# Four layer norms: squares summed around an early mean, drift taken out later, and the first two weight blocks behind each interleaved

## The chip, the cores and the metric

The kernel runs on one core of one Trainium2 chip. The metric is the device time of one execution in microseconds. The time of the kernel before is the median of three runs; the trace is that of one further execution, run with the hardware profiler.

## What is computed

Two transformer blocks over 512 tokens of width 1024, in float32. The change touches the four layer norms of the first block: one behind each mixer and one behind each feed-forward network, in two layers.

```python
def layer_norm(x, g, b):
    xf = x.astype(jnp.float32)
    mu = jnp.mean(xf, axis=-1, keepdims=True)
    var = jnp.mean(jnp.square(xf - mu), axis=-1, keepdims=True)
    y = (xf - mu) * lax.rsqrt(var + LN_EPS)
    return (y * g.astype(jnp.float32) + b.astype(jnp.float32)).astype(x.dtype)
...
    for i in range(DEPTH):
        ...
        x = layer_norm(ALPHA * x + y, ln_mix_g[i], ln_mix_b[i])
        f = conv_ffn(x, ffn_w_gate[i], ffn_w_up[i], ffn_conv_w[i], ffn_conv_b[i], ffn_w_down[i])
        x = layer_norm(ALPHA * x + f, ln_ffn_g[i], ln_ffn_b[i])
        x = x + jax.nn.sigmoid(x @ ple_w_gate[i]) * (p[i] @ ple_w_proj[i])
```

## The kernel before

**Layout.** The activations lie with features on partitions: 8 tiles (`KD`) of 128 features by 512 tokens (`S`). A sum over features is a matmul with a matrix of ones, which leaves the sum on all 128 partitions. Norms are numbered `i` = 0 to 3; even ones stand behind `mixout` (the mixer's output product, 8 blocks of weights) and before `gate`/`up` (the feed-forward's first products), odd ones behind `down` and before `pleproj`/`plegate`. `z` holds the tiles of an even norm, `z_ffn` those of an odd one; the latter lies on the same bytes as the low parts of `moving`.

**Precision.** Each float32 operand of a large product is split in a high and a low part (`moving_hi`/`moving_lo`, `w_hi`/`w_lo`), and `passes` (lines 696 to 698) multiplies three times: high by high, low by high, high by low. A weight block (128 by 1024) is 24 such passes of 512 columns. The matmuls with ones are plain float32; the profile shows each as two records.

**Who does what.** SyncE loads weight blocks into a ring of two slots (`ring`). GpSimd (POOL) splits each block in two halves (`split`, lines 2322 and 2325: `w_hi`, then `w_lo`), in the order of the blocks. It may overwrite the first half of a slot when TensorE has counted `half_done` for the block two before, and the second when it has counted `block_done`. TensorE (PE) runs all products in program order. ScalarE (ACT) and VectorE (DVE) take results out of the 8 PSUM banks. Each engine works through its own instructions in order and waits on semaphores; nothing is reordered.

**A norm.** VectorE's `residual` adds the scaled input to each output tile (line 1941, `z_ready`) and sums the first tiles on the way (line 1924: six in an even norm, four in an odd one). TensorE's `residual_norm` adds up the mean in bank 6 (line 865), VectorE's `norm` centres the eight tiles (line 1952), ScalarE squares them (line 1517), TensorE sums the squares in bank 7 (line 885), ScalarE takes the root (line 1380), VectorE inverts it (lines 1739 to 1742) and multiplies each tile with gain and inverse (line 1754). ScalarE writes the high part with the bias added (line 1522), VectorE the low part (line 1959), two tiles behind. When all eight are written, VectorE writes `x` back as high plus low (line 1968).

**Behind an even norm** TensorE runs `gate` and `up` blocks by turns, two per hidden tile. The first block waits for each tile's low part. VectorE splits `p` (line 1734), then works on the hidden tiles: two convolution steps (lines 1981, 1985) and the product (line 1990), which frees the banks for the next but one hidden tile. **Behind an odd norm** TensorE runs the first half of `pleproj` (it needs only `p`), five blocks of `plegate`, then the second half of `pleproj`, once VectorE has finished `x_ple` for four tiles (lines 2003, 2005). In layer 1 VectorE also makes the low parts of `gained` (line 2072) and adds squares for the next norm (line 1924) between them.

## Time and profile before

| what | value |
|---|---|
| median of 3 runs | 2598.41 us (2597.32 to 2599.71) |
| the profiled execution | 2594.23 us, its span 2592.4 us |
| mean granted TensorE clock | 0.979 |
| TensorE busy | 2473.3 us (95%) |
| VectorE busy | 1169.7 us (45%) |
| ScalarE busy | 688.6 us (27%) |
| GpSimd busy | 1898.8 us (73%) |

The four norms begin at about 336, 717, 1097 and 1478 us of the span. Times in the rows below are microseconds from the span's start. "Idle before" is how long the engine had stood idle, with what released it behind the arrow.

### The profile page before, as it was taken

The numbers are of one execution on the slowest core, as the hardware profiler recorded it, in microseconds if no ns is written. First come the engines' busy times: TensorE is split into PE (matmuls) and PEld (weight loads), VectorE is DVE, ScalarE is ACT, GpSimd is POOL, SyncE is SP. The second block draws the span as 40 slices with busy tenths as digits, with TensorE's granted clock in tenths as the row PEclk, the third lists the DMA queues.
The fourth block names the chain that finished last, engine by engine and source line by source line (L and its number), as shares of the span: only waits on it lengthen the run. The fifth ranks groups of instructions, "written<-read, shape, count | busy, mean of one in ns | idle before, by whom it ended". The sixth has DMA issues, their size and how long they took to land.

```text
span 2592.4 us, 32309 instructions
## 1 busy us (share of the span) xinstructions
PE 2473.3 (95%) x11170; PEld 1897.2 (73%) x11170; DVE 1169.7 (45%) x1541; ACT 688.6 (27%) x1244; POOL 1898.8 (73%) x1537
## 2 busy tenths in 40 slices
PE   7988989999989989999999999999999999999998
PEld 6745668888867853668888777866888878678886
DVE  7485463331061677463330176445423565553323
ACT  2264333330021138133330023145110131450101
POOL 8803368888867953678888778844999898449996
PEclk9989999999999999999999999899999999999999
DMA  4201012222212210112222223211222222112222
GB/s 170 89 1 41 33 65 98 96 97 97 98 63 94 94 51 1 61 66 96 94 96 97 89 72 107 86 58 41 98 98 97 89 98 81 49 50 101 93 97 90
DMA packets 57544, 207.08 MB, mean 80 GB/s; under 512 B 6512, under 2 KB 6896, under 8 KB 57200
## 3 DMA queue, kind: packets, MB, share of 16 engines
q1 hardware_dynamic: 55872, 199.87, 21.9%
q10 hardware_dynamic: 1584, 5.96, 0.6%
q8 instruction: 64, 1.05, 0.2%
q14 instruction: 24, 0.20, 0.0%
HBM read 203.71 MB, written 2.10 MB: 79 GB/s over the span
## 4 chain that ended last, share of the span: by engine, by line
PE 79%; DVE 11%; POOL 4%; issue 3%; ACT 2%; DMA 0%; POOLq 0%; DVEq 0%; ACTq 0%; SPq 0%
PE bank L696 22%; PE bank L697 21%; PE bank L698 21%; PE bank L771 3%; PE bank L726 3%; POOL w_hi L2322 2%; PE bank L820 2%; PE bank L799 2%; POOL w_lo L2325 2%; DVE region L1754 1%; PE bank L885 1%; DVE branch_lo L1734 1%; DVE moving_lo L1959 1%; PE bank L841 1%; DVE x L1968 1%
## 5 line engine op out<-in xcount | busy, mean ns | idle before, releaser
L2322 POOL TENSOR_TENSOR w_hi<-ring,unit 128x512 fp32r<-128x512 f32 x750 | 843.6, 1125 | 554.6 <-PE bank L698 417.1
L2325 POOL TENSOR_TENSOR w_lo<-ring,w_hi 128x512 fp32r<-128x512 f32 x750 | 1032.8, 1377 | 58.8
L696 PE MATMUL bank<-moving_hi,w_hi 128*128 128x512 f32 x1962 | 777.8, 396 | 29.9 <-DVE moving_lo L1959 18.8
L697 PE MATMUL bank<-moving_lo,w_hi 128*128 128x512 f32 x1962 | 771.6, 393 | 0.0
L698 PE MATMUL bank<-moving_hi,w_lo 128*128 128x512 f32 x1962 | 770.4, 393 | 0.0
L696 PEld LDWEIGHTS bank<-moving_hi,w_hi 128*128 128x128 f32 x1962 | 372.0, 190 | 125.0 <-issue 25.8
L698 PEld LDWEIGHTS bank<-moving_hi,w_lo 128*128 128x128 f32 x1962 | 372.6, 190 | 78.9
L697 PEld LDWEIGHTS bank<-moving_lo,w_hi 128*128 128x128 f32 x1962 | 372.6, 190 | 76.7 <-issue 1.2
L2269 DVE TENSOR_TENSOR region<-region,bank 128x512 f32<-128x512 f32 x64 | 39.7, 681 | 278.4 <-PE bank L698 278.4
L1941 DVE SCALAR_TENSOR_TENSOR region<-x,bank 128x512 f32<-128x512 f32 x32 | 21.3, 686 | 284.6 <-PE bank L698 284.5
L771 PE MATMUL bank<-region 64*128 64x512 f32 (+3 forms) x448 | 130.5, 601 | 15.6 <-DVE region L1728 4.4
L696 PE MATMUL bank<-hid_hi,w_hi 128*128 (+1 forms) x352 | 137.8, 391 | 0.0
L698 PE MATMUL bank<-hid_hi,w_lo 128*128 (+1 forms) x352 | 137.0, 389 | 0.0
L697 PE MATMUL bank<-hid_lo,w_hi 128*128 (+1 forms) x352 | 137.0, 389 | 0.0
L1690 ACT ACTIVATE region<-bank 128x512 f32<-128x512 f32 x64 | 38.1, 598 | 363.4 <-PE bank L698 363.4
L1795 DVE TENSOR_REDUCE negmax<-bank 128x2 f32<-128x256 f32 (+2 forms) x64 | 59.1, 923 | 113.7 <-PE bank L775 86.9
L1517 ACT ACTIVATE region<-region 128x512 f32<-128x512 f32 x32 | 19.3, 630 | 342.1 <-DVE region L1952 342.1
L1981 DVE SCALAR_TENSOR_TENSOR region<-bank,cols,region 128x511 f32<-128x511 f32 x44 | 32.9, 748 | 158.5 <-ACT region L1536 158.5
L1389 ACT ACTIVATE region<-bank 128x1024 f32<-128x1024 f32 (+2 forms) x80 | 66.6, 833 | 124.7 <-PE bank L820 124.6
L771 PEld LDWEIGHTS bank<-region 64*128 64x128 f32 (+1 forms) x448 | 41.8, 194 | 73.8 <-issue 50.9
L820 PE MATMUL bank<-tabs,work 128*128 128x128 f32 x496 | 72.2, 283 | 10.3 <-DVE work L1774 8.2
L820 PEld LDWEIGHTS bank<-tabs,work 128*128 128x128 f32 x496 | 56.2, 145 | 35.0 <-issue 25.2
(271 smaller groups left out, 3477.4 us busy)
## 6 DMA issues: line engine op xcount, KB each, us to landing
ring<-in_weights SPq DMA_DIRECT2D x375, 512.0 KB, 3.2
x<-in_x_t ACTq DMA_DIRECT2D x4, 512.0 KB, 8.4
out<-region SPq DMA_DIRECT2D x8, 256.0 KB, 2.2
region<-in_tables ACTq DMA_DIRECT2D x1, 1312.0 KB, 6.6
region<-in_tables ACTq DMA_DIRECT2D x1, 1024.0 KB, 5.6
region<-in_p_t ACTq DMA_DIRECT2D x2, 512.0 KB, 4.8
region<-in_tables SPq DMA_DIRECT2D x1, 320.0 KB, 10.1
small_w<-in_small_w ACTq DMA_DIRECT2D x1, 320.0 KB, 6.0
```

The costliest lines, as they stand in the source:

```text
L696: pe.matmul(bank, lhs[0], rhs[0], start=start, stop=False, skip_group_check=True)
L697: pe.matmul(bank, lhs[0], rhs[1], start=False, stop=False, skip_group_check=True)
L698: return pe.matmul(bank, lhs[1], rhs[0], start=False, stop=stop, skip_group_check=True)
L726: mm = pe.matmul(bank, cols_of(w, k * P, P)[p == 2], moved(k)[p == 1], start=(j == 0), stop=(j == 23), skip_group_check=True)
L771: mm = pe.matmul(at[c], q(u, c)[:, i * P:i * P + P], k(u, c)[:, 0:w], start=True, stop=True)
L799: mm = pe.matmul(out_bank(u)[HD * c:HD * c + HD, 2 * P * h + lo:2 * P * h + 2 * P], v(u, t, c), pt_half[:, h, c, t, lo:2 * P], start=(open ...
L820: mm = pe.transpose(psum[4 + c][:, kt * P:kt * P + P], prob[:, 2 * (t % 2) + c, kt * P:kt * P + P], ident)
L1389: act.activation(pt_half[:, i // 2, :, 0:kt, lo:lo + P], banks[:, 4:6, 0:kt * P].rearrange("p c (k q) -> p c k q", k=kt), ACT.Copy).then_i ...
L1795: dve.tensor_reduce(negmax[:, at:at + 2], banks[:, b:b + 2, 0:w], AX_X, ALU.max, negate=True).then_inc(maxed, 2)
L2269: ins = dve.tensor_tensor(t[:, i, :], t[:, i, :], psum[4 + i][:], ALU.mult)
L2322: pool.tensor_tensor(w_parts[0][:, s, at], ring[:, s, at], unit[:, 0:1].broadcast_to([P, BLK // 2]), ALU.mult).then_inc(split_hi, 1)
L2325: pool.tensor_tensor(w_parts[1][:, s, at], ring[:, s, at], w_parts[0][:, s, at].bitcast(F32), ALU.subtract).then_inc(split_ready, 1)
```

## The change

- **An early mean.** After four tiles (`EARLY`) TensorE spreads their sum over all partitions in bank 6 (`shift_of`; in an even norm between the fifth and sixth `mixout` block, in an odd one where the early mean stood before, inside `down`). VectorE subtracts a quarter of it, scaled to a mean, from all tiles (`shift`). Those tiles whose product isn't there yet are first filled by ScalarE with the scaled input (`scaled_ahead`), shifted, and get their product added when it comes (`add_product`): three in an even norm, four in an odd one.
- **Squares early.** ScalarE squares the shifted tiles, mostly into banks 4 and 5, and VectorE adds them up in `square_sum` (`add_squares`). TensorE then sums once over `square_sum` (in an even norm and over the last tile's square).
- **Drift.** The mean of the shifted tiles comes from bank 5. ScalarE copies it (`drift`) and squares it; VectorE takes the square from the mean of the squares (`variance`). VectorE centres four tiles (`centre`), GpSimd the other four (`recentre`), behind the split of two blocks of what follows.
- **Products in PSUM.** The product with gain and inverse goes to one of two banks (`scaled_bank`), from which ScalarE and VectorE make high and low part. A product waits for the low part made from its bank.
- **Two blocks at once.** `project_pair` runs the first two blocks behind the norm tile by tile. It counts `half_done` of both at the sixth tile. `down` counts `down_out` as each of three banks is finished. GpSimd's loop over the blocks is cut into pieces (`split_up_to`) to let `recentre` in.

```diff
-EARLY, EARLY_DOWN = 6, 4
+EARLY = 4
+CENTRED = 4
...
+        square_sum, late_sum, drift, drift_sq = (place(120 + 2 * j, S) for j in range(4))
+        square_late = place(0, 4, S)
...
+        def scaled_bank(i, n):
+            return psum[(4, 6, 2, 3)[2 * (i % 2) + n % 2]][:]
...
+            def project_pair(first, two_banks, ready):
+
+                w = [both(w_parts, np.s_[:, (first + h) % RING, :]) for h in range(2)]
+                for h in range(2):
+                    half_of(first + h, 0)
+                for k in range(KD):
+                    if k == KD // 2:
+                        for h in range(2):
+                            half_of(first + h, 1)
+                    pe.wait_ge(parts_ready, T["parts"][ready + (k,)])
+                    for h in range(2):
+                        mm = passes(two_banks[h], cols_of(w[h], k * P, P), moved(k), k == 0, k == KD - 1)
+                        if k == KD - 3:
+                            mm.then_inc(half_done, 1)
+                        if k == KD - 1:
+                            mm.then_inc(block_done, 1)
...
+            def shift_of(i):
 
                 pe.wait_ge(z_summed, i + 1)
-                add_mean(i, early_sum, first=True)
+                pe.matmul(psum[6][:], ones, early_sum, start=True, stop=True).then_inc(shift_ready, 1)
 
             def residual_norm(i):
 
+                pe.wait_ge(square_added, T["square_added"][(i, 3 if i % 2 else 6)])
                 if i % 2 == 0:
...
+                    pe.wait_ge(late_summed, i // 2 + 1)
+                    pe.matmul(psum[5][:], ones, late_sum, start=True, stop=False, skip_group_check=True)
+                for n in range(4 if i % 2 else KD - 1, KD):
                     pe.wait_ge(z_ready, KD * i + n + 1)
-                    mm = add_mean(i, (z_ffn if i % 2 else z)[:, n, :], last=(n == KD - 1))
+                    mm = pe.matmul(psum[5][:], ones, (z_ffn if i % 2 else z)[:, n, :], start=(i % 2 == 1 and n == 4),
+                                   stop=(n == KD - 1), skip_group_check=True)
                 mm.then_inc(mean_ready, 1)
...
-                sum_squares(("ln", i), psum[7], KD, lambda n: square[:, n, :])
+                if i % 2:
+                    pe.wait_ge(square_added, T["square_added"][(i, KD - 1)])
+                mm = pe.matmul(psum[7][:], ones, square_sum, start=True, stop=(i % 2 == 1), skip_group_check=True)
+                if i % 2 == 0:
+                    pe.wait_ge(squared, T["squared"][("ln", i, KD - 1)])
+                    mm = pe.matmul(psum[7][:], ones, square_late[:, 3, :], start=False, stop=True, skip_group_check=True)
...
+                    if n == 4:
+                        shift_of(i)
...
+                pe.wait_ge(hid_ready, KF * layer + 1)
+                project_pair(n0, (psum[0][:], psum[2][:]), ("ln", i - 1))
...
+                                if h == 1 and b == 6 and j == 1 and n < 3:
+                                    mm.then_inc(down_out, 1)
...
-                        pe.wait_ge(std_ready, T["std"][("ln", 2 * layer + 1)])
+                        pe.wait_ge(centered, CENTRED * (2 * layer + 2))
+                        pe.wait_ge(drift_ready, 2 * layer + 2)
                         project_p(layer, 0)
+                        project_pair(AT[("plegate", layer, 0)], (psum[0][:], psum[1][:]), ("ln", 2 * layer + 1))
...
+            def scaled_ahead(i):
+
+                tiles = z_ffn if i % 2 else z
+                act.wait_ge(block_done, done(("down", i // 2, 0, 0) if i % 2 else ("mixout", i // 2, 0)))
+                for n in range(direct(i), KD):
+                    act.activation(tiles[:, n, :], x[:, n, :], ACT.Copy, scale=ALPHA).then_inc(prescaled, 1)
+
             def norm_squares(i):
                 src = z_ffn if i % 2 else z
+                scaled_ahead(i)
+                through_bank = range(1, 4 if i % 2 else KD - 1)
                 for n in range(KD):
-                    act.wait_ge(centered, KD * i + n + 1)
-                    act.activation(square[:, n, :], src[:, n, :], ACT.Square).then_inc(squared, 1)
-                deviation(("ln", i), psum[7], D, col("eps_ln"), 0)
+                    if n < direct(i):
+                        act.wait_ge(shifted, T["shifted"][(i, n)])
+                    else:
+                        act.wait_ge(z_ready, KD * i + n + 1)
+                    if n == 0:
+                        dst = square_sum
+                    elif n in through_bank:
+                        if n >= 3:
+                            act.wait_ge(square_added, T["square_added"][(i, n - 2)])
+                        dst = psum[4 + n % 2][:]
+                    else:
+                        dst = square_late[:, n - 4, :]
+                    act.activation(dst, src[:, n, :], ACT.Square).then_inc(squared, 1)
+                act.wait_ge(mean_ready, i + 1)
+                act.activation(drift, psum[5][:], ACT.Copy, scale=1.0 / D).then_inc(drift_ready, 1)
+                act.wait_ge(drift_ready, i + 1)
+                act.activation(drift_sq, drift, ACT.Square).then_inc(drift_squared, 1)
+                act.wait_ge(variance, i + 1)
+                act.activation(std[:, 0, :], std[:, 1, :], ACT.Sqrt, bias=col("eps_ln")).then_inc(std_ready, 1)
...
+                    act.activation(moving[0][:, n, :], scaled_bank(i, n), ACT.Identity,
...
+            def shift(i, n):
+                tiles = z_ffn if i % 2 else z
+                return dve.scalar_tensor_tensor(out=tiles[:, n, :], in0=psum[6][:], scalar=-1.0 / (EARLY * P),
+                                                in1=tiles[:, n, :], op0=ALU.mult, op1=ALU.add)
+
+            def add_squares(i, n):
+                dve.wait_ge(squared, T["squared"][("ln", i, n)])
+                if n > 1:
+                    dve.wait_ge(square_added, T["square_added"][(i, n - 1)])
+                src = square_late[:, n - 4, :] if i % 2 and n >= 4 else psum[4 + n % 2][:]
+                dve.tensor_tensor(square_sum, src, square_sum, ALU.add).then_inc(square_added, 1)
+
             def residual(i):
 
                 layer = i // 2
-                for n in range(KD):
+                tiles = z_ffn if i % 2 else z
+
...
+                def add_product(n):
+                    dve.tensor_tensor(tiles[:, n, :], bank_of(n), tiles[:, n, :], ALU.add).then_inc(z_ready, 1)
+
+                for n in range(direct(i)):
+                    dve.scalar_tensor_tensor(out=tiles[:, n, :], in0=x[:, n, :], scalar=ALPHA, in1=bank_of(n),
                                              op0=ALU.mult, op1=ALU.add).then_inc(z_ready, 1)
...
+                dve.wait_ge(shift_ready, i + 1)
+                dve.wait_ge(z_ready, KD * i + direct(i))
+                for n in range(direct(i)):
+                    shift(i, n).then_inc(shifted, 1)
+                for n in range(direct(i), KD):
+                    dve.wait_ge(prescaled, T["prescaled"][(i, n)])
+                    ins = shift(i, n)
+                link(ins)
+                if i % 2:
+                    for n in range(1, 4):
+                        add_squares(i, n)
+                    for n in range(4, KD):
+                        add_product(n)
+                    for n in range(4, KD):
+                        add_squares(i, n)
+                    return
+                add_squares(i, 1)
+                add_squares(i, 2)
+                add_product(5)
+                add_squares(i, 3)
+                dve.wait_ge(z_ready, KD * i + 6)
+                link(dve.tensor_tensor(late_sum, z[:, 4, :], z[:, 5, :], ALU.add))
+                add_squares(i, 4)
+                add_squares(i, 5)
+                add_product(6)
+                dve.wait_ge(z_ready, KD * i + 7)
+                dve.tensor_tensor(late_sum, late_sum, z[:, 6, :], ALU.add).then_inc(late_summed, 1)
+                add_squares(i, 6)
+                add_product(7)
...
+                    dve.scalar_tensor_tensor(out=lo, in0=scaled_bank(i, n), scalar=col(bias, KD * (i // 2) + n),
+                                             in1=hi.bitcast(F32), op0=ALU.add, op1=ALU.subtract).then_inc(parts_ready, 1)
...
+                dve.wait_ge(drift_ready, i + 1)
+                dve.wait_ge(z_ready, KD * i + KD)
+                early = 1 if i % 2 else 2
+                for n in range(early):
+                    centre(n)
+                dve.wait_ge(drift_squared, i + 1)
+                dve.wait_ge(summed, T["summed"][("ln", i)])
+                dve.scalar_tensor_tensor(out=std[:, 1, :], in0=psum[7][:], scalar=1.0 / D, in1=drift_sq, op0=ALU.mult,
+                                         op1=ALU.subtract).then_inc(variance, 1)
+                for n in range(early, CENTRED):
+                    centre(n)
+                dve.wait_ge(std_ready, T["std"][("ln", i)])
+                inverse(rstd[:, 0, :], std[:, 0, :], slice(0, P))
+                dve.wait_ge(centered, CENTRED * (i + 1))
+                for n in range(KD):
+                    if n >= 2:
+                        lower_biased(n - 2)
+                        dve.wait_ge(parts_ready, T["parts"][("ln", i, n - 2)])
+                    if n >= CENTRED:
+                        dve.wait_ge(recentered, (KD - CENTRED) * i + n - CENTRED + 1)
+                    dve.scalar_tensor_tensor(out=scaled_bank(i, n), in0=t[:, n, :], scalar=col(gain, KD * (i // 2) + n),
+                                             in1=rstd[:, 0, :], op0=ALU.mult, op1=ALU.mult).then_inc(normed, 1)
+                lower_biased(KD - 2)
+                lower_biased(KD - 1)
...
+            def recentre(i):
+                tiles = z_ffn if i % 2 else z
+                pool.wait_ge(drift_ready, i + 1)
+                for n in range(CENTRED, KD):
+                    pool.tensor_tensor(tiles[:, n, :], tiles[:, n, :], drift, ALU.subtract).then_inc(recentered, 1)
...
+            at = RING
+            for key, between in ((("gate", 0, 0), lambda: recentre(0)), (("pleproj", 0, 0), lambda: recentre(1)),
+                                 (("mixout", 1, 0), lambda: scale_first([u for u in UNITS if u[0] == "C"])),
+                                 (("gate", 1, 0), lambda: recentre(2)), (("pleproj", 1, 0), lambda: recentre(3))):
+                split_up_to(at, AT[key] + RING)
+                at = AT[key] + RING
+                between()
+            split_up_to(at, len(BLOCKS))
```

Three places in the order of instructions. VectorE, norm 0, from the last output tiles to the first low part (`region` holds `z`; `work` the sum of the first tiles), before:

```order
L1941 SCALAR_TENSOR_TENSOR region<-x,bank 128x512 x2
L1952 SCALAR_TENSOR_TENSOR region<-bank,region 128x512 x8
L1739 STREAM_TRANSPOSE rstd<-std 128x512
L1741 RECIPROCAL inverse_tmp<-rstd 128x16
L1742 STREAM_TRANSPOSE rstd<-inverse_tmp 128x512
L1754 SCALAR_TENSOR_TENSOR region<-region,cols,rstd 128x512 x3
L1959 SCALAR_TENSOR_TENSOR moving_lo<-region,cols,moving_hi 128x512
```

and now, from the last product that is added (line 2039):

```order
L2039 TENSOR_TENSOR region<-bank,region 128x512
L2082 SCALAR_TENSOR_TENSOR region<-bank,region 128x512 x2
L2098 SCALAR_TENSOR_TENSOR std<-bank,region 128x512
L2082 SCALAR_TENSOR_TENSOR region<-bank,region 128x512 x2
L1817 STREAM_TRANSPOSE rstd<-std 128x512
L1819 RECIPROCAL inverse_tmp<-rstd 128x16
L1820 STREAM_TRANSPOSE rstd<-inverse_tmp 128x512
L2111 SCALAR_TENSOR_TENSOR bank<-region,cols,rstd 128x512 x2
L2088 SCALAR_TENSOR_TENSOR moving_lo<-bank,cols,moving_hi 128x512
```

Four of the eight centrings are gone, a variance stands between them, and the first low part comes after two products instead of three. The same place on TensorE, the matmuls with ones behind the last `mixout` block, before:

```order
L865 MATMUL bank<-work,tabs 128x512
L865 MATMUL bank<-region,tabs 128x512 x2
L885 MATMUL bank<-region,tabs 128x512 x8
```

and now:

```order
L911 MATMUL bank<-region,tabs 128x512
L914 MATMUL bank<-region,tabs 128x512
L919 MATMUL bank<-region,tabs 128x512
L922 MATMUL bank<-region,tabs 128x512
```

Eleven have become four; one more (line 904) has moved ahead of the last three blocks. GpSimd, at the end of the second `up` half that is split before the norm, has now:

```order
L2473 TENSOR_TENSOR w_hi<-ring,unit 128x512
L2476 TENSOR_TENSOR w_lo<-ring,w_hi 128x512
L2498 TENSOR_TENSOR region<-region 128x512 x4
L2473 TENSOR_TENSOR w_hi<-ring,unit 128x512
L2476 TENSOR_TENSOR w_lo<-ring,w_hi 128x512
```

The four subtractions of `recentre` stand between two splits that followed each other before.

## Rows read from the trace of the kernel before

**Rows 1.** The page: chain that ended last, share of the span by engine
```profile
PE 79%; DVE 11%; POOL 4%; issue 3%; ACT 2%; DMA 0%; POOLq 0%; DVEq 0%; ACTq 0%; SPq 0%
```

**Rows 2.** The chain behind norm 0, in order of time: start us, us, what
```profile
365.31 8.07 DVE x L1968 x5
373.38 1.98 DVE p_lo L1734
```

**Rows 3.** VectorE's timeline, norm 0: start us, us, line, op, out<-in, count, idle before
```profile
336.45 0.69 DVE L1941 SCALAR_TENSOR_TENSOR region<-x,bank 128x512 f32<-128x512 f32 x1 [4.76 <-PE bank L698]
339.03 4.87 DVE L1952 SCALAR_TENSOR_TENSOR region<-bank,region 128x512 f32<-128x512 f32 x8 [1.89 <-PE bank L865]
...
350.10 2.08 DVE L1754 SCALAR_TENSOR_TENSOR region<-region,cols,rstd 128x512 f32<-128x512 f32 x3
...
358.72 2.07 DVE L1959 SCALAR_TENSOR_TENSOR moving_lo<-region,cols,moving_hi 128x512 fp32r<-128x512 f32 x3
360.83 12.55 DVE L1968 TENSOR_TENSOR x<-moving_hi,moving_lo 128x512 f32<-128x512 f32 x8
```

**Rows 4.** TensorE's timeline, norm 0
```profile
340.43 7.13 PE L885 MATMUL bank<-region,tabs 128*128 128x512 f32 x16 [1.44 <-ACT region L1517]
...
352.99 0.77 PE L696 MATMUL bank<-moving_hi,w_hi 128*128 128x512 f32 x1 [5.42 <-DVE moving_lo L1959]
...
378.68 0.47 PE L696 MATMUL bank<-moving_hi,w_hi 128*128 128x512 f32 x1 [0.46 <-DVE region L1990]
```

**Rows 5.** ScalarE's timeline, norm 0
```profile
344.58 1.28 ACT L1380 ACT_TABLE_LOAD   x1
347.61 0.69 ACT L1380 ACTIVATE std<-bank,cols 128x512 f32<-128x512 f32 x1 [1.74 <-PE bank L885]
```

**Rows 6.** GpSimd's timeline, norm 0
```profile
358.48 3.22 POOL L2322 TENSOR_TENSOR w_hi<-ring,unit 128x512 fp32r<-128x512 f32 x1 [19.60 <-PE bank L698]
361.77 1.62 POOL L2325 TENSOR_TENSOR w_lo<-ring,w_hi 128x512 fp32r<-128x512 f32 x1
...
364.92 1.62 POOL L2325 TENSOR_TENSOR w_lo<-ring,w_hi 128x512 fp32r<-128x512 f32 x1
```

**Rows 7.** VectorE's timeline, norm 1
```profile
717.17 2.48 DVE L1941 SCALAR_TENSOR_TENSOR region<-x,bank 128x512 f32<-128x512 f32 x4 [54.60 <-PE bank L698]
...
732.73 2.08 DVE L1754 SCALAR_TENSOR_TENSOR region<-region,cols,rstd 128x512 f32<-128x512 f32 x3
734.73 1.53 DVE L1959 SCALAR_TENSOR_TENSOR moving_lo<-region,cols,moving_hi 128x512 fp32r<-128x512 f32 x1
...
737.88 1.52 DVE L1959 SCALAR_TENSOR_TENSOR moving_lo<-region,cols,moving_hi 128x512 fp32r<-128x512 f32 x1
...
748.89 8.79 DVE L1968 TENSOR_TENSOR x<-moving_hi,moving_lo 128x512 f32<-128x512 f32 x8
```

**Rows 8.** TensorE's timeline, norm 1: `pleproj`, a tile of `plegate`, second `pleproj`
```profile
731.02 0.48 PE L696 MATMUL bank<-p_hi,w_hi 128*128 128x512 f32 x1 [0.82 <-issue]
...
741.81 0.79 PE L696 MATMUL bank<-moving_hi,w_hi 128*128 128x512 f32 x1 [1.35 <-DVE moving_lo L1959]
...
772.54 0.40 PE L696 MATMUL bank<-p_hi,w_hi 128*128 128x512 f32 x1
```

**Rows 9.** All of one line: ns min/median/max, first and last start
```profile
L1754 DVE SCALAR_TENSOR_TENSOR bank<-x,cols,bank x16: 743/747/756, 1567.9 to 2087.9; 128x512 f32<-128x512 f32 x16
...
L2003 DVE TENSOR_TENSOR bank<-region,bank x16: 681/696/697, 757.6 to 1556.3; 128x512 f32<-128x512 f32 x16
```

**Rows 10.** Stages: us, busy us (count) of PE, PEld, DVE, ACT, POOL; clock, DMA
```profile
353.00:357.90 4.90, 4.90 (x12) 3.31 (x12) 4.90 (x8) 2.56 (x4) 0.00 (x0) 0.50 0.00 0
741.80:750.90 9.10, 8.66 (x19) 5.47 (x20) 9.07 (x12) 3.50 (x5) 2.71 (x2) 0.52 0.15 55
750.90:772.60 21.70, 21.70 (x98) 17.95 (x97) 12.13 (x13) 2.39 (x4) 20.28 (x16) 1.00 0.27 97
```

**Rows 11.** VectorE's timeline, norm 3: a low part of `gained`
```profile
1524.79 1.58 DVE L2072 SCALAR_TENSOR_TENSOR gained_lo<-x,cols,gained_hi 128x512 fp32r<-128x512 f32 x1
```

103 lines of the change are left out of this document (54 added, 49 removed).

## The prediction

> **What bounds the kernel now.** I read the page first: its chain of waits [rows 1] runs over TensorE for 79% of the span and over VectorE for 11%. So an edit pays only where TensorE stands still for VectorE. The chain over the stretch behind the first norm shows where: it runs not over matmuls but over VectorE, down to the write-back of `x` and the low part of `p` [rows 2]. Then the timelines of the four norms, engine by engine: norms 0 and 2 stand between `mixout` and `gate`, norms 1 and 3 between `down` and `plegate`; 2 repeats 0 and 3 repeats 1 to within 0.1 us. What counts is what is late at the end of each.
>
> Norm 0. The last `mixout` block ends at 336.42 (VectorE takes it at 336.45 [rows 3]). Call this zero. Centring begins at +2.6, the 16 records of the eight squares' sums take TensorE 7.13 us from +4.0, the deviation is out at +11.9, the first product with the gain starts at +13.7 and TensorE, after 5.42 us of waiting, starts `gate` at +16.6 [rows 3 to 5]. But that is not the end. VectorE ends its last low part at +24.4, writes `x` back in 12.55 us because GpSimd splits weights beside it, and hands over the first hidden product only at +42.0. TensorE has done four blocks and waits 0.46 us for exactly that, starting the fifth at 378.68 [rows 3, 4]; the chain goes the same way [rows 2]. From there on it is steady. **A norm 0 or 2 is worth what VectorE's whole row of work moves up, not what the first matmul moves up.**
>
> Norm 1. Zero is 717.14. First product at +15.6, low parts done at +31.7, `x` at +40.5 [rows 7]. TensorE does half of `pleproj` from +13.9, is held tile by tile, and starts the second half of `pleproj` at +55.4 [rows 8]. Here TensorE is last, not VectorE.
>
> **Part 1: squares summed early (norms 0, 2).** Removed behind zero: six of the eight square sums, two of three mean matmuls, eight centrings before the first square. One fp32 matmul is two records, 7.13 / 8 = 0.89 us [rows 4]. Added before zero, on VectorE: eight shifts at 0.61 (4.87 / 8 [rows 3]), six square sums and three products at 0.69, two sums of tiles. That is 4.9 + 6.2 + 1.7 = 12.8 us, spread over the last three blocks of 5.44 us, so it ends some 3 us before zero; TensorE's three blocks cover it. Not covered is the matmul that spreads the early mean: before, it ran while TensorE waited for the last tile anyway; now it stands between two blocks: **+0.86**. New chain behind zero: last product 0.03 + 0.69; its mean matmul 1.05 (+1.8); the drift's copy on ScalarE 0.63 (+2.4), two centrings 1.3 beside its square and two square matmuls (+4.4); variance 0.72; deviation 0.70 [rows 5]. Two more centrings end at +5.7 beside the deviation; transpose, reciprocal, transpose 1.8 (348.30 to 350.10 [rows 3, 5]). First product at +7.5, or +8.4 with the 0.86, against +13.7: **5.3 us earlier**. The table load of 1.28 us [rows 5] comes right after the drift's square and lies beside the variance; uncovered it would cost at most 0.6.
>
> **Part 2: products through PSUM.** Sixteen operations for eight tiles, as before, but each product now waits for the low part before it. Back to back they overlap: three in 2.07 us at 0.75 each, 0.66 apart [rows 3]; the wait takes away that overlap, 0.11 per tile, **+0.9 us** a norm. I take it as real, since the low part must have been written before its bank is free. The low part now has one SBUF input. Beside a splitting GpSimd, operations with two SBUF inputs stretch (L1959 to 1.52 [rows 7]), those with one in PSUM don't (L2003: 697 ns at most in 16 [rows 9]), so it is immune. A PSUM output costs nothing (747 ns [rows 9]).
> The Trainium skill says otherwise in "Perfetto Trace Analysis", section Optimizing Scalar/DVE Operations: about 125 ns of access overhead on PSUM against 60 on SBUF for VectorE. By it the sixteen operations would lose 1.0 us a norm, 4 us in all; the row with the PSUM output shows no difference, so the sum leaves it out.
>
> **Part 3: recentring on GpSimd.** Four subtractions at 1.3 to 1.6 us [rows 6], behind splits that are done; GpSimd stands idle for 19.6 us there [rows 6]. They run from +2.4 to about +8.4, VectorE needs the first at +13. Nothing. If they were late, VectorE's tile five would wait.
>
> **Part 4: two blocks interleaved.** Four blocks take 21.7 us [rows 10], 5.44 each and 0.227 a pass. Per contraction tile the pair has 6 passes, 1.36, about VectorE's pace of 1.44. Before, the first block went at VectorE's pace and the second (5.44) came after. But GpSimd, with a ring of two, may split the next block only from tile 5 of the pair, and beside VectorE's write-back it needs 3.15 us for half a block [rows 6] where TensorE needs 2.72. Norm 0: pair from +10.5 with a slow clock at first (half speed for 4.9 us cost ten passes, 2.3 us) to +23.8; GpSimd is released at +20.6 and the next five halves at 3.15 keep TensorE to +36. The write-back starts at +20.0, 12.25 us; then `p` and the convolution as before (373.38 to 378.42, 5.0 [rows 2, 4]): product at +37.3 against +42.0. TensorE is there 1.4 us earlier and waits. **Norms 0 and 2: 4.7 us each, 9.4** (5.3 - 0.9, and 0.3 from the first write-back, which GpSimd does not yet hamper; hence the interleaving itself brings nothing here). Bounds 3.6 (write-back held throughout, one product stretched by 0.8 behind a recentring) to 6.5 (no cost of the wait, the first two tiles of the write-back undisturbed).
>
> **Norms 1 and 3.** Zero is the end of `down`. Three banks are now taken over before the end; the four mean matmuls still run after it, to +3.6. The four late squares are summed from SBUF: two beside GpSimd's last split, done +4.8; their matmul +5.9; variance +6.6; three centrings +8.5; first product +10.3, against +15.6. `pleproj` now waits for the centrings and starts at +8.5 instead of +13.9. The tiles: two or three stretched by the split of the second `plegate` block, low parts done at +24.1. The pair ends at +28.7. Then three blocks at TensorE's pace with 0.5 us lost to GpSimd: +45.4, against +55.4: **10.0 for norm 1** (12.5 at full clock, 8 if two more tiles are stretched).
> Norm 3 has VectorE's additional work: the write-back ends at +36.7; then four times two operations (5.3), two low parts of `gained` at 1.58 [rows 11] and one sum of squares, also from two SBUF inputs, at about the same before the fourth `x` that `pleproj` waits for: +46.6 against +55.4: **8.8** (bounds 7 and 11), the same at either clock.
>
> **Sum**: 9.4 + 10.0 + 8.8 = 28.2 us. Against the profiled execution, 2594.2 (span 2592.4 and 1.8 around it), that is 2566.0. The median of the three runs lies 4.2 above it, so **2570**. The bounds give 22.2 (2 x 3.6 + 8 + 7) to 36.5 (2 x 6.5 + 12.5 + 11): 2562 to 2576.
>
> **Rivals.** (a) *GpSimd's refill sets the pace.* If the pair's release comes in effect at its end, the next halves follow at 3.15 each: the fifth block after norm 0 starts 2 us later than above, norms 1 and 3 reach the second `pleproj` at about +50. Gain 2 x 2.7 + 2 x 5.4 = 16: 2582. For: the ring has no third slot, and after norm 0 the splits ran at 3.15 in the kernel before too [rows 6]. Against: the release stands at tile 5, 3.5 us before the end.
> (b) *Slower.* The tile chain, 16 operations a norm, is held by GpSimd's use of SBUF: at 737.88 one tile takes 3.15 us [rows 7]. If PSUM operands don't protect and GpSimd is busy through the chain, 32 tiles lose 1.7 us each, 54 us: 2624. It decides from 17 tiles on. For: the four subtractions read SBUF, and a split took 3.22 [rows 6]. Against: [rows 9], and GpSimd is held back until tile 5.
> (c) *No change: half clock lasts.* TensorE loses the squares' sums, which kept it busy, and stands still for 6.6 us before `gate` instead of 5.4 [rows 4]. At half clock a microsecond gives half a microsecond of work; to use up 28 us it would take 14 us more of it after each norm, besides the 1.4 us of slack at norms 0 and 2. That is 2598. For: after norm 1 half clock held for 9.1 us. Against: after norm 0 it was granted back after 4.9 [rows 10], with TensorE as busy as it would be now.
> (d) *More*: full clock everywhere and the write-back undisturbed: 2560. The Trainium skill ("TensorE: Matmul & The Clock Gate", Part 1: The HAM clock gate) states that the throttled state is the default and activity releases it. By that alone (c) ends as soon as the pair is busy.
>
> **Chances.** Forecast 0.68, (a) 0.17, (b) 0.05, (c) 0.05, (d) 0.05. The range takes in the bounds, (d) and most of (a): 2560 to 2584. A measurement tells 0.2% (5 us) from no change: faster 0.90, same 0.05, slower 0.05.
>
> **What would show it.** First product at +8.4 and +10.3 behind the last block; low parts with a PSUM input at 0.75 beside a busy GpSimd; TensorE's fifth block after norms 0 and 2 waiting for VectorE's hidden product; after norm 1 no such wait, after norm 3 one for `x`; half clock in `pleproj`. Waits of TensorE for `w_lo` of more than 1 us a block mean (a); products of 1.7 us all along mean (b).

## The result, and the profile after

The changed kernel takes 2571.5 us (median of 4 runs, 2566.3 to 2572.7), the kernel before 2598.3 (4 runs, 2597.3 to 2599.7): ratio 0.989, 95% interval 0.988 to 0.991. The forecast was 2570 with a range of 2560 to 2584. The profiled execution took 2566.3 with a span of 2564.5, which is 27.9 less than the span before.

Here and in every run below a **zero** is 0.23 us behind the start of a stage's last matmul (the end of `mixout` for norms 0 and 2, of `down` for norms 1 and 3). "Fifth block" is the start of TensorE's fifth block behind a zero, "second pleproj" that of the second half of `pleproj`. The stage from the zero of norm 0 to that of norm 1 is the safest measure of norm 0, because it ends where TensorE has long run without a wait.

| us | before | after | moved |
|---|---|---|---|
| zero 0 to zero 1 | 380.73 | 374.72 | -6.0 (-5.1 with the shift matmul that now lies ahead of the zero) |
| norm 1: second pleproj | +55.56 | +46.60 | -9.0 |
| zero 2 to zero 3 | 380.70 | 374.37 | -6.3 (-5.5) |
| norm 3: second pleproj | +55.72 | +47.67 | -8.0 |

That is 27.6 in all. The rest of the span nets 0.3: some 2.7 less ahead of norm 0 and 2.8 more behind norm 3, where the work is the same. The granted clock differs there in the same sense: ahead of norm 0 TensorE stood at 1.2 GHz for 20.5 us instead of 27.3, behind the second `pleproj` of norm 3 for 44.9 instead of 36.3.

The page of the changed kernel, the chain by engine, to be set beside [rows 1]: VectorE has 9% instead of 11%, GpSimd 7% instead of 4%.
```profile
PE 77%; DVE 9%; POOL 7%; issue 4%; ACT 2%; DMA 0%; POOLq 0%; DVEq 0%; ACTq 0%; SPq 0%
```
VectorE, norm 0 of the changed kernel, zero at 334.44 (start us, us, line, operation, out<-in, count, idle before); [rows 3] is the same place before:
```profile
334.64 0.69 DVE L2039 TENSOR_TENSOR region<-bank,region 128x512 f32<-128x512 f32 x1 [3.21 <-PE bank L719]
...
341.95 1.44 DVE L2111 SCALAR_TENSOR_TENSOR bank<-region,cols,rstd 128x512 f32<-128x512 f32 x2
...
352.19 1.60 DVE L2088 SCALAR_TENSOR_TENSOR moving_lo<-bank,cols,moving_hi 128x512 fp32r<-128x512 f32 x2
353.82 11.57 DVE L2119 TENSOR_TENSOR x<-moving_hi,moving_lo 128x512 f32<-128x512 f32 x8
365.32 2.30 DVE L1812 TENSOR_TENSOR p_lo<-region,p_hi 128x1024 fp32r<-128x1024 f32 x1
...
369.99 0.69 DVE L2141 TENSOR_TENSOR region<-region,bank 128x512 f32<-128x512 f32 x1 [0.80 <-ACT region L1618]
```
And TensorE there, as [rows 4]:
```profile
344.38 0.77 PE L717 MATMUL bank<-moving_hi,w_hi 128*128 128x512 f32 x1 [6.15 <-DVE moving_lo L2088]
...
370.84 0.49 PE L717 MATMUL bank<-moving_hi,w_hi 128*128 128x512 f32 x1 [1.18 <-DVE region L2141]
```
The first product starts at +7.5. TensorE still waits at its fifth block for the same hidden product as before (1.18 us instead of 0.46): the write-back of 11.57 us stands between the last low part and it.

VectorE, norm 1, zero at 709.16 ([rows 7] before):
```profile
707.32 2.74 DVE L2039 TENSOR_TENSOR region<-bank,region 128x512 f32<-128x512 f32 x4 [34.34 <-PE bank L719]
709.97 5.31 DVE L2018 TENSOR_TENSOR region<-region 128x512 f32<-128x512 f32 x4
...
720.74 1.42 DVE L2111 SCALAR_TENSOR_TENSOR bank<-region,cols,rstd 128x512 f32<-128x512 f32 x2
...
727.39 1.01 DVE L2111 SCALAR_TENSOR_TENSOR bank<-region,cols,rstd 128x512 f32<-128x512 f32 x1
728.32 0.74 DVE L2088 SCALAR_TENSOR_TENSOR moving_lo<-bank,cols,moving_hi 128x512 fp32r<-128x512 f32 x1
...
733.10 7.70 DVE L2119 TENSOR_TENSOR x<-moving_hi,moving_lo 128x512 f32<-128x512 f32 x8
```
TensorE, norm 1 ([rows 8] before):
```profile
715.34 1.13 PE L919 MATMUL bank<-region,tabs 128*128 128x512 f32 x2 [2.58 <-DVE region L2018]
719.16 0.77 PE L717 MATMUL bank<-p_hi,w_hi 128*128 128x512 f32 x1 [2.69 <-issue]
...
727.94 0.48 PE L717 MATMUL bank<-moving_hi,w_hi 128*128 128x512 f32 x1 [0.66 <-POOL w_lo L2476]
```
TensorE by stretches of norm 1 (us, busy us and count, granted clock, DMA share, GB/s); [rows 10] is before:
```profile
709.30:719.10 9.80, 4.58 (x11) 0.91 0.16 54
719.10:724.20 5.10, 5.04 (x12) 0.50 0.00 0
724.20:727.90 3.70, 3.08 (x13) 1.00 0.00 0
```
GpSimd, norm 1: the drift taken out of four tiles, and its next free start after the pair:
```profile
713.47 5.39 POOL L2498 TENSOR_TENSOR region<-region 128x512 f32<-128x512 f32 x4 [1.35 <-ACT region L1592]
...
735.80 1.30 POOL L2473 TENSOR_TENSOR w_hi<-ring,unit 128x512 fp32r<-128x512 f32 x1 [4.80 <-PE bank L719]
```
The four late square adds last 5.31 us, twice the 2.74 of the four adds above them, which read a bank. TensorE stands still for 2.58 us, for those adds, and for 2.69 us. The second wait is marked "issue", but by the program it is for the four centrings (with eight of them, in e5 below, it is 5.09). Then TensorE runs `pleproj` at 1.2 GHz (0.50). The low part that reads a bank takes 0.74 us beside GpSimd, a product that reads tile and `rstd` from SBUF 1.01.

At norm 3 the clock fell earlier, 6.4 us behind the zero instead of 8.2, and took in the matmul over the squares. That one took 1.91 us instead of 1.13, and `pleproj` started at +10.8 instead of +10.0:
```profile
1461.29 1.91 PE L919 MATMUL bank<-region,tabs 128*128 128x512 f32 x2 [2.58 <-DVE region L2018]
1465.89 0.77 PE L717 MATMUL bank<-p_hi,w_hi 128*128 128x512 f32 x1 [2.69 <-issue]
```

### The profile page after: what moved, and what is told of

It is laid out like the page before. It is cut to its first block, busy times and chain, and to the rows that moved or that the text cites. A ratio compares the mean times of both kernels' runs of the same rounds, so it can differ in the third digit from the quotient of the medians.

```text
span 2564.5 us, 32275 instructions
## 1 busy us (share of the span) xinstructions
PE 2449.4 (96%) x11118; PEld 1888.2 (74%) x11118; DVE 1187.4 (46%) x1587; ACT 701.3 (27%) x1266; POOL 1913.4 (75%) x1553
## 3 DMA queue, kind: packets, MB, share of 16 engines
q1 hardware_dynamic: 55872, 199.87, 22.3%
## 4 chain that ended last, share of the span: by engine, by line
PE 77%; DVE 9%; POOL 7%; issue 4%; ACT 2%; DMA 0%; POOLq 0%; DVEq 0%; ACTq 0%; SPq 0%
PE bank L717 21%; PE bank L719 21%; PE bank L718 21%; POOL w_hi L2473 4%; PE bank L809 3%; PE bank L764 3%; POOL w_lo L2476 3%; PE bank L837 2%; PE bank L858 2%; DVE branch_lo L1812 1%; PE bank L879 1%; DVE work L1852 1%; DVE moving_lo L1812 1%; ACT region L1682 0%; PE bank L1209 0%
## 5 line engine op out<-in xcount | busy, mean ns | idle before, releaser
L2042 DVE SCALAR_TENSOR_TENSOR region<-x,bank 128x512 f32<-128x512 f32 x18 | 12.2, 687 | 150.4 <-PE bank L719 150.3
L1590 ACT ACTIVATE region<-region 128x512 f32<-128x512 f32 x14 | 8.8, 631 | 265.5 <-DVE region L2010 183.6
```

## The experiments

All medians stand against runs of the kernel before on the same chip (its medians there: 2596.0 for e1 to e4, 2597.3 for e5 to e8, 2595.0 for e9 to e12). The column "gain" is what a median lies below the kernel before on its own chip, and kernels are compared by it. Stages that no edit touches scatter too: from the second `pleproj` of layer 0 to zero 2 they took between 324.5 and 329.2 us in these profiles, largely with the clock (13.7 us at half clock in the shortest, 27.3 in the longest). A (1) marks a median of a single run. So a part is judged by the marks of its own stage, and the totals only where they differ by more.

The marks of one profile each scatter as well. At norms 1 and 3 the changed kernel, e4 and e10 have the same code. The first `pleproj` started between +10.0 and +10.95 there, late where the clock fell at +5.8 to +6.6 and early where it fell at +8.2 or later, and the second between +46.6 and +47.7. At norms 1 and 3 less than 1.1 us therefore tells nothing. At norm 2 the changed kernel, e3 and e6 have the same code and took 374.4, 377.1 and 374.7.

| | median | gain | zero 0 to 1 | 2nd pleproj, norm 1 | zero 2 to 3 | 2nd pleproj, norm 3 |
|---|---|---|---|---|---|---|
| after | 2571.5 | 26.8 | 374.7 | +46.6 | 374.4 | +47.7 |
| e1 serial | 2572.5 | 23.5 | 375.5 | +47.1 | 377.0 | +46.5 |
| e2 pair alone | 2589.0 | 7.0 | 380.6 | +50.7 | 380.3 | +52.5 |
| e3 filler | 2569.2 | 26.8 | 374.7 | +44.5 | 377.1 | +46.3 |
| e4 late write-back | 2564.5 | 31.5 | 373.0 | +47.5 | 373.4 | +46.6 |
| e5 centring on VectorE | 2578.1 (1) | 19.2 | 377.1 | +47.2 | 377.1 | +47.8 |
| e6 squares in PSUM | 2564.6 | 32.7 | 374.7 | +43.8 | 374.7 | +44.0 |
| e7 e4, release earlier | 2567.5 | 29.8 | 373.3 | +46.8 | 372.7 | +47.5 |
| e8 together | 2559.4 | 37.8 | 373.4 | +43.1 | 372.8 | +43.5 |
| e9 serial, filler | 2576.4 (1) | 18.5 | 375.5 | +47.1 | 377.1 | +47.1 |
| e10 SBUF products | 2570.4 (1) | 24.6 | 373.9 | +47.5 | 373.6 | +46.9 |
| e11 one filler, two centrings | 2563.8 | 31.2 | 373.9 | +44.9 | 373.4 | +45.2 |
| e12 e11 with e10 | 2566.9 | 28.1 | 375.8 | +44.9 | 375.3 | +45.2 |

**e1, what the interleaving is worth in the changed kernel.**
```diff
-                for k in range(KD):
...
-                    for h in range(2):
-                        mm = passes(two_banks[h], cols_of(w[h], k * P, P), moved(k), k == 0, k == KD - 1)
+                for h in range(2):
...
+                    for k in range(KD):
...
+                        mm = passes(two_banks[h], cols_of(w, k * P, P), moved(k), k == 0, k == KD - 1)
```

> The changed kernel with the interleaving undone at all four norms: the two weight blocks run one after the other again, and the first block gives its half free after its fourth tile. Theory: the interleaving is worth next to nothing here. Norms 0 and 2: the fifth block waits for VectorE, whose write-back starts when the low parts are ready, which doesn't depend on the order of TensorE's blocks: it stays at +36.2 after the norm's zero (within 0.7). Norms 1 and 3: at half clock TensorE trails the low parts anyway, so the second pleproj stays at +46.4 and +47.5 (within 1). Total within 3 us of the changed kernel, that is 2568 to 2575. Rival: the interleaving saves half a block (2.8 us) at each norm, since a single block waits for each tile (1.45 us a tile against 0.69 us of matmuls): the marks move by +2.8 each, total +11 us (2583).

Total 2572.5, ratio to the kernel before 0.991 (0.988 to 0.993), not to be told from the changed kernel. By its marks the interleaving gives 0.8 and 2.7 us at norms 0 and 2; the 0.5 that it gives at norm 1 and the 1.1 that it costs at norm 3 are within the scatter. So it is small, about 3 us in all, but at norm 2 as large as the rival said. There the waits tile by tile of the first block brought the clock down a second time:
```profile
1101.50:1107.50 6.00, 3.78 (x12) 0.92 0.00 0
1107.50:1113.00 5.50, 5.50 (x21) 0.78 0.14 39
```
At norm 0, with the same waits but for one of 0.25 us, it stayed at 1.00; e9, which has this code too, repeats both (stages of 375.5 and 377.1). The 2.7 is less sure than it looks, since the interleaved code itself took 377.1 at norm 2 in e3. At norms 1 and 3 the pair uses up its own gain: it needs two blocks split before it starts (+18.8 and +19.6), a single block starts at +17.5 and +18.0.

**e2, the interleaving alone, in the kernel before.** The diff's `project_pair`, used in `feed_forward` and `per_layer` as in the change, and nothing else.

> The kernel before with the interleaving alone. Theory: fifth block after norms 0 and 2 within 0.7 us of +43.6 (VectorE's write-back is last there too), second pleproj after norms 1 and 3 within 1.5 us of +55.4 (half clock until nine us after the first block's start hides the tile pace): total within 4 us of the kernel before, so that squares summed early carry the whole gain of 27 us. Rival: 2.8 us a norm, total 2587.

2589.0, ratio 0.997 (0.996 to 0.998): 7 us faster, where I had expected none. Norms 0 and 2 as expected (0.1 and 0.4). At norm 1 the second `pleproj` came 4.8 us earlier, at norm 3 3.3. The half clock of 9.1 us in [rows 10], which I had taken to hide the order, hangs on the order: with the order alone changed, the same stretch (from 24.8 us behind the zero) runs at full clock.
```profile
740.50:749.60 9.10, 9.10 (x40) 1.00 0.16 54
```
By the gains, everything but the interleaving gives 23.5 (e1), the interleaving alone 7.0, both together 26.8: at norms 1 and 3 they save partly the same time. No run has the early squares alone, without the banks and GpSimd's share of the centring; e5 and e10 below price those two.

**e3, is it the clock that ends norms 1 and 3?**
```diff
+            def filler(count):
+                for _ in range(count):
+                    pe.matmul(psum[6][:], ones, early_sum, start=True, stop=True)
...
                 if i % 2:
+                    filler(3)
                     pe.wait_ge(square_added, T["square_added"][(i, KD - 1)])
...
                 mm.then_inc(summed, 1)
+                if i % 2:
+                    filler(3)
```

> The changed kernel with three spare matmuls (ones against the early sum, 0.86 us each, into a bank that nobody reads any more) before the wait for the last square add and three behind the matmul of the squares, at norms 1 and 3 only: TensorE is busy where it waited. Theory: the first pleproj then runs at full clock (5.6 us instead of 8), gives its half free 2.6 us earlier to GpSimd, whose split starts the interleaved pair: the pair ends and the second pleproj starts 2.6 us earlier at norm 1 (+43.8) and about 3 at norm 3 (+44.5, where VectorE's x is then as late as TensorE); total 5 to 6 us less, 2566. Rival 1: the clock falls in spite of them: marks as they were or up to 1.7 us later (two fillers that run past the end of the wait). Rival 2: the pair is held by GpSimd's split or the low parts, whose times don't follow: under 1 us.

The clock is 1.00 through `pleproj`, the pair starts at +16.0 instead of +18.8 and +19.6, the second `pleproj` comes 2.1 earlier at norm 1 and 1.4 at norm 3, to within the scatter. At norm 3 it now waits 1.59 us for VectorE's `x`, because GpSimd, let go earlier, splits beside the write-back. The same happens at norm 1:
```profile
735.85 12.48 DVE L2126 TENSOR_TENSOR x<-moving_hi,moving_lo 128x512 f32<-128x512 f32 x8
```
That is the length which the prediction gave the write-back of norm 3 (+24.1 to +36.7); it came true only here. The total doesn't show the gain: the four runs lie between 2564.1 and 2575.3, and the profiled one is the slowest. It lost 2.7 us in the stage of norm 2, whose code is unchanged. There the write-back took 12.71 us instead of 10.74, TensorE waited for the hidden product behind it, and the clock fell for 3.4 us:
```profile
1104.68 12.71 DVE L2126 TENSOR_TENSOR x<-moving_hi,moving_lo 128x512 f32<-128x512 f32 x8
1122.57 0.79 PE L717 MATMUL bank<-moving_hi,w_hi 128*128 128x512 f32 x1 [2.65 <-DVE region L2148]
```

**e4, is VectorE's write-back last at norms 0 and 2?**
```diff
-                for n in range(KD):
-                    hi, lo = both(moving, np.s_[:, n, :])
-                    dve.tensor_tensor(x[:, n, :], hi.bitcast(F32), lo.bitcast(F32), ALU.add)
+                for n in range(KD if i % 2 else 0):
+                    write_back(n)
...
+                for par in range(2):
+                    hidden(0, par)
+                    for n in range(4 * par, 4 * par + 4):
+                        write_back(n)
```

> The changed kernel with VectorE's eight adds that write x back after norms 0 and 2 moved behind the first two hidden tiles (four behind each), and the low part of p behind them; nothing left out. Theory: the write-back is what ends last before the fifth block, by itself (370.7 at norm 0) and through GpSimd, whose half splits take 3.15 us beside it and 2.4 alone. Without it TensorE goes on at its own pace: fifth block at +32.0 to +33.5 instead of +36.2, so 3 to 4 us less at norm 0 and as much at norm 2, total 6 to 8 us less (2564). Rival: GpSimd's refill, started 12 us late, sets the pace by itself, and the fifth block moves by under 1 us a norm (total 2570).

Fifth block at +33.6 and +34.1 instead of +36.4 and +36.2, without a wait: VectorE's row was last at norm 0. At norm 2, where the changed kernel's TensorE had not waited at that block but 0.63 us for `w_lo` just before it, the write-back held it through GpSimd. Of the 2.8 and 2.1 us, 1.7 and 1.0 remain at the next zero. The rest goes to GpSimd, whose splits are stretched by the write-back later on, and for which TensorE then waits at the eighth block:
```profile
385.70 0.50 PE L717 MATMUL bank<-moving_hi,w_hi 128*128 128x512 f32 x1 [0.63 <-POOL w_lo L2487]
```
So theory and rival are both partly right. The gain is 4.7 us larger than the changed kernel's, of which the marks of norms 0 and 2 explain 2.7.

**e5, the recentring's share** (`CENTRED = 8`).

> The changed kernel with CENTRED = 8: VectorE takes the drift out of all eight tiles, GpSimd out of none. Theory: the share that GpSimd takes costs nothing where it lies and saves VectorE four operations of 0.6 us in the chain before the inverse: first product 2.4 us later (+9.7 at norm 0, +13.8 at norm 1), fifth block 2.4 later (+38.8), second pleproj 2.4 later (+49.0); total +8 to +10. Rival: TensorE or GpSimd ends last at those marks, and they move by less than 1 us.

Norms 0 and 2 exactly so: fifth block at +38.8, stages 377.1 (+2.4 and +2.7). Norms 1 and 3 not: first `pleproj` 1.4 and 0.6 later, the second 0.6 and 0.1, within the scatter. Without GpSimd's subtractions the late adds took 4.29 instead of 5.31, and TensorE had room. So by this one profile the recentring on GpSimd is worth 5 us, all of it at norms 0 and 2.

**e6, the late squares in PSUM.**
```diff
+                    elif i % 2:
+                        if n == KD - 1:
+                            act.wait_ge(square_added, T["square_added"][(i, 4)])
+                        dst = late_bank(n)
...
-                src = square_late[:, n - 4, :] if i % 2 and n >= 4 else psum[4 + n % 2][:]
+                src = late_bank(n) if i % 2 and n >= 4 else psum[4 + n % 2][:]
```

> The changed kernel where, at norms 1 and 3, ScalarE writes the last four squares into PSUM banks 4, 6 and 7 that are free by then, instead of SBUF, so that VectorE's four late adds read one operand from SBUF instead of two. Theory: the adds took 5.3 us instead of 2.7 because both operands lie in SBUF while GpSimd splits weights there: now 2.7 to 3.2 us, TensorE's wait of 2.58 us for them is gone, the first pleproj at +7.6 to +8.0 instead of +10.0 to +10.8, the second one 2.4 us earlier at both norms if the half clock stays, up to 5 earlier if the clock doesn't fall; total -5 (2566). Rival: the adds are held by ScalarE's squares (squares 6 and 7 wait for a bank) and still take over 4.5 us.

```profile
710.10 3.07 DVE L2026 TENSOR_TENSOR region<-bank,region 128x512 f32<-128x512 f32 x4
```
```profile
717.05:720.70 3.65, 3.65 (x10) 0.55 0.00 0
```
3.07 us instead of 5.31, first `pleproj` at +7.8 at both norms, the second 2.8 and 3.7 earlier, median 2564.6. The second operand in SBUF was the cost. Half clock stayed, but shorter: the first 3.65 us of `pleproj` (the second row, TensorE) have 0.55, what follows 0.99. One gap of 2.69 us was enough for it; the other had shrunk to 0.34.

**e7, releasing GpSimd earlier** (with e4).
```diff
-                        if k == KD - 3:
+                        if k == KD // 2 - 1:
```

> The late write-back of e4 and, at all four pairs, the two blocks' first halves given free to GpSimd after the fourth tile (k = 3) instead of the sixth. Theory: in e4 GpSimd's refill is what is left: it starts 12 us late and TensorE waits 0.95 us for it at the eighth block; started 2.8 us earlier it doesn't make TensorE wait: from the zero of norm 0 to that of norm 1 372.0 instead of 373.0, norm 2 the same. Rival: GpSimd beside the last low parts stretches VectorE's products (0.76 to 1.01 each) and the fifth block comes 0.5 to 1 later than in e4 (33.6), which gives the gain back.

No effect: the two stages together 746.1, in e4 746.4, and TensorE waits at the eighth block as before (0.66 us for `w_lo`), though GpSimd started its split at norm 0 at +17.3 instead of +19.7. That is one half of a block only: the next half needs the whole block counted, and started at +22.7, in e4 at +22.3. So the release could not have given much. What VectorE does beside GpSimd holds it there. The products weren't stretched enough to cost anything either.

**e8, together.** The edits of e3, e4, e6 and e7, and in `per_layer`:
```diff
+                    if n < 4:
+                        write_back(n + 4)
```

> Together: the late write-back and the earlier release (e7), the late squares in PSUM (e6), the spare matmuls at norms 1 and 3 (e3, into bank 0), and at norms 1 and 3 only the first four tiles of x written back before the per-layer products, the other four each behind one of the first four products, so that x for the second pleproj isn't held by eight adds. Theory: parts add: norms 0 and 2 2 to 3 us less than the changed kernel each, second pleproj at +42.0 to +42.5 at norm 1 and +42.5 at norm 3: total 13 to 15 us less, 2557. Rival: at norms 1 and 3 GpSimd's split or the tile chain ends last and the gains of e3 and e6 overlap: second pleproj at +44, total 2561.

2559.4, ratio 0.986 (0.984 to 0.987): the fastest of all, 38 us below the kernel before and by the gains 11 better than the changed one. The second `pleproj` lies between theory and rival (+43.1, +43.5): with the adds no longer late, the six spare matmuls themselves hold the first one (+9.7, in e6 +7.8).

**e9, why was the interleaving worth more before?** The edits of e1 and e3.

> The interleaving undone (as in e1) and the spare matmuls of e3 at norms 1 and 3. Asks why the interleaving saved 4.8 and 3.3 us at norms 1 and 3 in the kernel before (e2) and nothing in the changed one (e1). Theory: it saves there by keeping TensorE from waiting tile by tile, after which the clock falls; in the changed kernel the clock has fallen before, at the first pleproj, whatever follows. With the spare matmuls that first fall is gone (e3), so the order matters again: here plegate's first block waits tile by tile, the clock falls there, and the second pleproj is 3 to 5 us later than in e3: +47.5 to +49.5 at norm 1 against +44.5. Rival: the interleaving is worth nothing once norms are short: +44.5 within 1.

+47.1 at both norms, 2.6 and 0.8 later than e3. The size at norm 1 is near the theory's lower end, but its reason is wrong: the clock did not fall behind the waits (TensorE by stretches):
```profile
725.70:733.00 7.30, 5.35 (x20) 1.00 0.21 72
```
What is lost is the waiting itself: four waits of 0.49 to 0.81 us and whatever shorter ones lie between. So the order is worth up to half a block at full clock, and more where waits also bring the clock down, which they did in the kernel before and at norm 2 of e1 and e9, but not at norms 1 and 3 of e9 and not at norm 0 of either.

**e10, the price of the banks.**
```diff
-            return psum[(4, 6, 2, 3)[2 * (i % 2) + n % 2]][:]
+            return psum[2 + n % 2][:] if i % 2 else z[:, n, :]
...
+                        if i % 2:
+                            dve.wait_ge(parts_ready, T["parts"][("ln", i, n - 2)])
```

> The changed kernel with the scaled tiles of norms 0 and 2 left in SBUF, in place, and without the wait that guards the two banks. Theory: the wait and not the bank costs: tile pace 1.33 us instead of 1.45, low parts 0.9 us earlier, fifth block at +35.5 instead of +36.4; norms 1 and 3 as they were; total -2. Rival: GpSimd's earlier start or VectorE's write-back fills it again: +36.2 or more.

Fifth block at +35.7 and +35.5, stages 0.8 and 0.7 shorter, in a single run. At norm 0 a tile takes 1.33 us instead of 1.45 and the write-back starts 0.7 earlier, so the wait costs somewhat less than the 0.9 that the prediction charged. The bank itself costs nothing that can be seen: a product takes 0.76 us into a bank and 0.75 into SBUF. At norms 0 and 2 GpSimd stands still while the tiles are made, so the banks protect nothing there and are a small loss.

**e11 and e12, one spare matmul and more for GpSimd** (e8 with `filler(1)` behind the squares only and `CENTRED = 2`; e12 with e10's edit).

> e8 with one spare matmul behind the matmul of the squares and none ahead of it (in e8, with the adds no longer late, the spare matmuls were what the first pleproj waited for: +9.7 against +7.8 in e6), and CENTRED = 2, so that VectorE takes the drift out of two tiles and GpSimd out of six. Theory: first pleproj at +6.6 (two operations of 0.6 less ahead of it), second one at +41.0 to +42.0 at norms 1 and 3, norms 0 and 2 0.3 us less than in e7; total 2556. Rival: GpSimd's six tiles (7.4 us) hold back its split for the pair at norms 1 and 3: second pleproj at +43 or more.

> e11 with the scaled tiles of norms 0 and 2 in SBUF, as in e10. Theory: there TensorE is last now, and its pair ends with the low parts: 0.9 us less at norms 0 and 2 each, total 2 us less than e11. Rival: GpSimd's refill is last at the eighth block and takes it back: same as e11 within 0.5 us a norm.

Both slower than e8. The first `pleproj` starts at +6.6, as said, but the pair then waits 3.55 us for GpSimd, which recentres six tiles first (+15.9): the rival. And at norms 0 and 2 VectorE's first products now run beside that recentring. First e11, then e12, where the low part reads SBUF too:
```profile
342.10 2.73 DVE L2129 SCALAR_TENSOR_TENSOR bank<-region,cols,rstd 128x512 f32<-128x512 f32 x2
344.75 0.74 DVE L2106 SCALAR_TENSOR_TENSOR moving_lo<-bank,cols,moving_hi 128x512 fp32r<-128x512 f32 x1
```
```profile
344.45 1.75 DVE L2106 SCALAR_TENSOR_TENSOR moving_lo<-region,cols,moving_hi 128x512 fp32r<-128x512 f32 x1
```
Two products in 2.73 us instead of 1.44. The low part takes 0.74 from a bank and 1.75 from SBUF. So e12's pair starts 1.0 us later than e11's. The clock then comes back later too (TensorE from the start of the pair until then, first e11, then e12):
```profile
345.63:349.60 3.97, 3.97 (x9) 0.50 0.00 0
```
```profile
346.35:352.28 5.93, 5.93 (x14) 0.50 0.00 0
```
Two more microseconds at half clock cost 1.0. Together that is the 1.9 us by which e12 is worse than e11 in either stage, where e10 alone gained 0.8.

## Why the prediction was right

In this section marks count from the prediction's zero, which lies 0.17 us later than that of the tables.

**Norms 0 and 2: right, by its own steps.** With the 0.86 of the shift matmul the hidden product was to be ready at +37.3; it was at +36.9 (370.68). Gain 5.1 and 5.5 by stages against 4.7. First product forecast +8.4, measured +8.2. At norm 0 TensorE waits for VectorE at the fifth block, as said. At norm 2 it doesn't wait there: 0.63 us for `w_lo` just before is a near tie with GpSimd. e4 shows that the write-back was last at both, e5 that the recentring is hidden there, e10 the wait's price (0.7 to 0.8 instead of 0.9) and that a bank as output costs nothing. The write-back took 11.57 and 10.74, not 12.25. **"The interleaving itself brings nothing here"** is right only in part: 0.8 and 2.7 (e1), the larger one with a fall of the clock which the sum didn't have.

**Norm 1: gain 9.0 against 10.0.** The term that was mis-sized is "two beside GpSimd's last split, done +4.8": four adds beside GpSimd's split and its recentring took 5.31 us and were done at +5.9. Everything behind moved with it (first product +11.4 against +10.3, `pleproj` +9.8 against +8.5), and e6 took it away. The half clock in `pleproj` came, but for 5.1 us instead of 8. That made up for most of the late start: the first `pleproj` ended at +18.0 against +17.7, by luck. e3 shows that the half clock costs 2.1 us at the second `pleproj`, where the prediction's bound had 2.5. Low parts done at +23.7 against +24.1 (later start, fewer tiles stretched); pair end +29.6 against +28.7.

**Norm 3: gain 8.0 against 8.8, and its last step was wrong.** The write-back was to take 12.6 us (+24.1 to +36.7) and make VectorE last, with the fourth `x` at +46.6. It took 7.69, because GpSimd, held until the sixth tile of a pair that ran late, stood still for its first 2.7 us (at norm 1 until 735.80, above):
```profile
1479.83 7.69 DVE L2119 TENSOR_TENSOR x<-moving_hi,moving_lo 128x512 f32<-128x512 f32 x8
```
The fourth `x` was there at +44.1. TensorE was last, at +47.5, late by the late adds and the half clock. VectorE was 2.5 us earlier than forecast, TensorE 2.1 later than the +45.4 that the sum gives it at norm 1. The two nearly cancelled, so the near hit at norm 3 is luck. The statement "the same at either clock" was wrong too: in e3 full clock gave 1.4, and only then did VectorE hold TensorE up.

**The account of the kernel before was wrong in one place** that the sum didn't lean on: the half clock there (9.1 us) looked like a cost that the order of blocks couldn't touch, and e2 removed it by the order alone.

**Rivals.** (a) didn't happen as a whole: release at tile six sufficed, and releasing earlier, which moves one half only, changed nothing (e7). It shows on a small scale: at norms 1 and 3 the pair waits 0.66 and 0.30 us for `w_lo` and starts 1.3 and 1.6 later than e1's single block, and TensorE waits at e4's eighth block. (b) was refuted in the changed kernel, by low parts of 0.74 beside GpSimd. Its mechanism is real where both inputs are in SBUF (late adds, e11, e12). (c) TensorE worked at half clock for 4.4 to 5.8 us behind each of the four norms, not 14 more. (d) wasn't reached by the changed kernel (fastest run 2566.3).

Sum of the stages 27.6 against 28.2. What stays open: why nearly equal waits brought the clock down at norm 2 of e1 and e9 and not at norm 0, what makes the clock fall early at one odd norm and late at another, and what each part but the interleaving, the recentring and the banks is worth by itself.

## What to carry to other kernels

Ask of every step behind a barrier which engine's row ends last at the next meeting point, and take the rows of work that are merely queued there (a write-back, a cast) out of it: e4 moved the fifth block by 2.8 and 2.1 us with that alone. Put one operand of each VectorE operation that runs beside a busy GpSimd into a PSUM bank; where GpSimd stands still, the bank protects nothing and the wait for it costs (e10). Shortening a chain opens new gaps in front of TensorE; look at the granted clock behind them, and check a filler again once the gap is gone.

## What the runs showed of the hardware

- VectorE's operations with both tile inputs in SBUF stretch beside GpSimd's elementwise work: adds 5.31 us for four against 3.07 with one from a bank, a low part 1.75 against 0.74, eight write-backs 12.48 against 7.70 with GpSimd idle for the first 2.7. Nothing with one input from a bank did: in the 14 profiles 4539 operations on 128x512 with an input from a bank lay mostly beside GpSimd's elementwise work, and the longest took 0.76 us; with two tile inputs from SBUF the longest took 1.85. The Trainium skill ("SBUF — State Buffer", section SBUF: two separate sides) states that a VectorE operation with two SBUF inputs and a GpSimd operation that reads SBUF share one pair of ports, which one of them holds for its whole length; these rows agree.
- GpSimd loses as well: half a block's split takes 2.4 us alone and 3.15 beside the write-back.
- TensorE's clock fell to 1.2 GHz in or behind two gaps of 2.58 and 2.69 us, also where the first was only 0.34 (e6), and did not with spare fp32 matmuls in them (e3). With gaps of 0.34 and 0.64 (e11) it stayed up until the wait of 3.55 us that came next.
- In one stage with the same code profiles differed by 4.6 us, along with the time that the clock stood at 1.2 GHz (13.7 us in the profile of 324.5, 23.9 to 27.3 in the six of 328.8 to 329.2), while at norm 0 three kernels with the same code took 374.72 to 374.73: marks next to an edit tell more than the totals, where the clock fell alike.
